# Entries of two blocks: the norm before the first block's second layer done by pairs of tiles, transposes by token tiles, and weight splits put elsewhere in the engines' orders

## The chip, the cores and the metric

One Trainium2 chip, one of its cores. The metric is device time in microseconds (us) of one execution; lower is better. The kernel before took 3221.67 us (median of 3 runs, 3217.72 to 3221.87).

## What is computed

Two blocks of two layers each, all on 512 tokens of width 1024 (four tiles of 128 tokens) and, in the first block, 256 context tokens more (tiles 4 and 5). Cut to what matters here:

```python
def first_block_layer(x, ctx):                       # twice
    h = rms_norm(x, g) * (1 + scale) + shift         # per layer, scale and shift from c (ctx likewise)
    p = h @ w_in                                     # queries, keys, values, gates, ...
    x = x + gate * (mixer(p) @ w_out)

def second_block_layer(x):                           # twice
    y = hybrid_mixer(x, ...)                         # compressed, latent and forgetting attention
    x = layer_norm(DN_ALPHA * x + y, ln_g[l, 0], ln_b[l, 0])
    y = memory_cross_attention(x, mem, xa_w_q[l], xa_w_kv[l], xa_w_o[l])
    x = layer_norm(DN_ALPHA * x + y, ln_g[l, 1], ln_b[l, 1])
    y = square(relu(x @ mlp_w_up[l])) @ mlp_w_down[l]
    x = layer_norm(DN_ALPHA * x + y, ln_g[l, 2], ln_b[l, 2])
```

All products are made at nearly full fp32 precision out of rounded fp32 parts: an operand is split into a high part (rounded) and a low part (the rest), and three products (high high, high low, low high) are added (`acc3`, L346).

## The kernel before

It is written by hand with semaphores. Each engine runs its own list of instructions in the order in which the Python code issues them; `wait_ge` makes an engine wait for a count. Most steps are functions with one part per engine (`tensor`, `dve`, `act`, `pool`), so what is issued earlier in the code comes earlier on every engine.

**Weights** come in `chunks` of up to 1 MB, loaded by SP into two raw slots in turn (`sp_chunks`, L337), each when the raw slot was freed two chunks before. A chunk is then split into high and low parts: ACT copies the rounded high part (`act_split`, L287), DVE subtracts for the low part (`dve_split`, L294), and that frees the raw slot. TensorE waits for the low part (`pe.wait_ge(*tw)`). Where the splits stand in the orders of ACT and DVE is set by `take()` (splits the chunk if that wasn't done, and the next one), `split_next()` and `plan_split`.

**Entry of a layer of the first block.** `normed` scales the tokens by their root mean square: squares on ACT, a square root on ACT, a reciprocal root made exact by small steps on DVE (L448 to L456), and six scalings of 128x1024 on DVE (L488). `modulated` transposes them by 128x128 blocks (L598) and adds scale and shift, writing `hT` as a high part (ACT L607; for the context tokens DVE L633) and a low part (DVE: L635, or L627 and L630 for every second k). It goes over the 8 k-blocks outside and over token tiles 0 to 3 and context tiles 4 and 5 inside. Then `project3` begins with `w_in`. In the first layer the projections wait for the last low part (`pe.wait_ge(*t_hT)`, L1688). In the second layer there stands a chain: `out_proj` of the first layer (its last column part n = 3 goes over six tiles: TensorE L887, DVE product with the gate L903, POOL sum L923, ACT square L917), then `barrier()` (every engine waits for all), the store of `X` to `x_rows` by POOL (L2153), `normed` for all six tiles at once, `split_next()`, `modulated`, another `barrier()` (L2180) and the first projection (L2182). `h1_low` lies where `X` lay, so DVE waits for the store before the first low part (L2173).

**Second block.** `residual` is the layer norm by token tiles; the product groups of what comes next may begin behind it (`FirstHalves`). At the second layer's start the keys' projection (`project3_T(..., begun=...)`, L2869) finishes what was begun; its evacuations are L2454 on DVE and L2462 on ACT, POOL then copies halves of the keys (L2874), and DVE's `blocks(0)` (L2909, L2915) waits for these copies before the queries' chunk is split by the next `take()`. **Memory attention** (`MemoryTiles`) is interleaved with the second residual of each layer; ahead of it stands the projection of its queries (L3560), and ahead of the evacuations of that projection stands the split of the first `mlp_w_up` chunk, issued by `FirstHalves()` through `take(False)`.

Of the kernel before, what the change touches and what calls it, by code (L numbers as in the profile page):

```python
# [8 lines left out]
F32 = mybir.dt.float32  # L9
# [85 lines left out]
def program(nc, D, out):  # L95
# [369 lines left out]
    def normed(xn, junk, loaded, squared=None):  # L465

        have = squared is not None
        squared = squared or ac.next()
# [3 lines left out]
        def act():  # L472
            a.wait_ge(*loaded)
            for t in [] if have else range(6):
# [106 lines left out]
    def modulated(l, hT, xn, tmp, ready, t_mod):  # L581
# [4 lines left out]
        for k in range(8):  # L586
            for c, ts in ((0, range(4)), (1, range(4, 6))):
                b = bank()
                work.append((k, c, ts, b, psum_free[b], mm.next(), ac.next(), dv.next()))
                psum_free[b] = work[-1][7]  # L590

        def tensor():
            for tok in ready:
                pe.wait_ge(*tok)
            for k, c, ts, b, free, full, value, low in work:
                pe.wait_ge(*free)
                for n, t in enumerate(ts):
                    m = pe.transpose(PS[:, b, n * 128:n * 128 + 128], xn[:, t, k * 128:k * 128 + 128], ident[:, :])  # L598
                m.then_inc(*mm.up())

        def act():
            a.wait_ge(*t_mod)
            for i, (k, c, ts, b, free, full, value, low) in enumerate(work):
                n = len(ts) * 128
                a.wait_ge(*full)
# [5 lines left out]
                if i >= len(tmp):  # L611
                    a.wait_ge(*work[i - len(tmp)][7])
                a.activation(tmp[i % len(tmp)][:, 0:n], PS[:, b, 0:n], ACT.Identity, bias=aff[l][:, k, c, 1:2],
                             scale=aff[l][:, k, c, 0:1]).then_inc(*al.event())

        def dve():
            v.wait_ge(*t_mod)
            for k in range(8):
                for i in (2 * k, 2 * k + 1):
                    c = i % 2  # L620
                    n = len(work[i][2]) * 128
                    v.wait_ge(*work[i][6])
                    if c == 0 and k % 2:
                        b, x = work[i][3], tmp[i % len(tmp)][:, 0:n]
                        if i >= len(tmp):
                            v.wait_ge(*work[i - len(tmp)][7])
                        v.scalar_tensor_tensor(x, PS[:, b, 0:n], aff[l][:, k, 0, 0:1], hT[0][:, k, 0:n].bitcast(F32),  # L627
# [3175 lines left out]
```

## Time and profile before

| | |
|---|---|
| median of 3 runs | 3221.67 us (3217.72, 3221.67, 3221.87) |
| profiled execution, its own time | 3218.43 us |
| its span | 3216.6 us |
| mean granted TensorE clock | 0.962 of full |
| TensorE matmul busy | 2932.8 us (91%) |
| DVE, ACT, POOL busy | 1666.1 (52%), 1068.4 (33%), 446.9 us (14%) |
| DMA | 262.00 MB, mean 81 GB/s |

A row of the timeline has the start in us from the span's start, the busy us, the engine, the line, the operation with its output and inputs, and in brackets the idle time of the engine just before, with what ended it. A duration is up to 0.1 us longer than the distance to the next row of the same engine, since consecutive instructions overlap. "PE" is TensorE's matmul, "S" the large SBUF tensor in which most data lies, "HL" the split weights, "PS" PSUM.

### The profile page before, as it was taken

The numbers are of one execution on the slowest core, as the hardware profiler recorded it, in microseconds if no ns is written. First come the engines' busy times: TensorE is split into PE (matmuls) and PEld (weight loads), VectorE is DVE, ScalarE is ACT, GpSimd is POOL, SyncE is SP. The second block draws the span as 40 slices with busy tenths as digits, with TensorE's granted clock in tenths as the row PEclk, the third lists the DMA queues.
The fourth block names the chain that finished last, engine by engine and source line by source line (L and its number), as shares of the span: only waits on it lengthen the run. The fifth ranks groups of instructions, "written<-read, shape, count | busy, mean of one in ns | idle before, by whom it ended". The sixth has DMA issues, their size and how long they took to land. (4 is left out here: it accounts for less than half of the span.)

```text
span 3216.6 us, 43502 instructions
## 1 busy us (share of the span) xinstructions
PE 2932.8 (91%) x17412; PEld 2349.5 (73%) x17412; DVE 1666.1 (52%) x3168; ACT 1068.4 (33%) x1869; POOL 446.9 (14%) x400
## 2 busy tenths in 40 slices
PE   5789989997997898999998899998899999899998
PEld 2378874787984486476888689897556688778988
DVE  6845656853577744835235542425564533653334
ACT  3333335123135521634222431311353422332231
POOL 3200013321004520402020000000131111000000
PEclk8999999998999999999999899999899999999999
DMA  5433220232223043012223222222211233132221
GB/s 166 144 123 105 92 73 1 79 92 82 73 86 56 25 113 89 1 60 66 94 84 131 66 92 93 92 92 64 66 41 33 73 99 112 53 105 92 89 94 67
DMA packets 245407, 262.00 MB, mean 81 GB/s; under 512 B 12802, under 2 KB 227954, under 8 KB 245080
## 3 DMA queue, kind: packets, MB, share of 16 engines
q1 hardware_dynamic: 227808, 203.93, 21.0%
q0 software_dynamic: 12528, 45.08, 4.0%
q10 hardware_dynamic: 4872, 10.21, 1.5%
q8 instruction: 140, 2.29, 0.3%
q14 instruction: 59, 0.48, 0.0%
HBM read 245.04 MB, written 13.11 MB: 80 GB/s over the span
## 5 line engine op out<-in xcount | busy, mean ns | idle before, releaser
L346 PE MATMUL PS<-xT,HL 128*128 128x512 f32 (+2 forms) x3552 | 800.2, 387 | 23.2 <-DVE HL L294 15.0
L294 DVE TENSOR_TENSOR HL<-S,HL 128x2048 fp32r<-128x2048 f32 (+1 forms) x204 | 422.8, 2078 | 723.4 <-ACT HL L287 721.6
L346 PEld LDWEIGHTS PS<-xT,HL 128*128 128x128 f32 (+1 forms) x3552 | 650.2, 189 | 166.0 <-DVE HL L294 16.3
L287 ACT ACTIVATE HL<-S 128x2048 fp32r<-128x2048 f32 (+1 forms) x204 | 351.4, 1728 | 732.7 <-PE PS L3620 280.1
L3620 PE MATMUL PS<-HL,hd 128*128 128x256 f32 x3072 | 377.4, 286 | 11.3 <-DVE hd L3611 11.2
L3620 PEld LDWEIGHTS PS<-HL,hd 128*128 128x128 f32 x3072 | 375.9, 195 | 13.4 <-DVE hd L3611 12.9
L1189 ACT ACTIVATE S<-S,S 128x256 f32<-128x256 f32 (+5 forms) x292 | 189.2, 648 | 210.6 <-DVE S L1130 203.3
L1224 POOL TENSOR_SCALAR S<-S,S 128x512 f32<-128x512 f32 (+4 forms) x104 | 179.0, 1721 | 419.1 <-DVE S L1145 250.0
L1092 PEld LDWEIGHTS PS<-S,S 128*128 128x128 f32 (+1 forms) x1048 | 114.5, 141 | 146.2 <-issue 39.7
L1092 PE MATMUL PS<-S,S 128*128 128x128 f32 (+1 forms) x1048 | 171.3, 291 | 44.6 <-DVE S L1158 15.9
L346 PE MATMUL PS<-h_high,HL 128*128 128x512 f32 (+1 forms) x768 | 201.2, 348 | 0.1
L346 PE MATMUL PS<-HL,h_high 128*128 128x256 f32 x1024 | 188.4, 287 | 11.7 <-DVE S L2179 5.9
L1079 PE MATMUL PS<-S 64*128 64x256 f32 (+6 forms) x736 | 162.6, 514 | 30.7 <-DVE S L1130 27.8
L346 PEld LDWEIGHTS PS<-HL,h_high 128*128 128x128 f32 x1024 | 162.7, 195 | 12.2 <-issue 6.1
L1079 PEld LDWEIGHTS PS<-S 64*128 64x128 f32 (+1 forms) x736 | 73.1, 201 | 121.6 <-DVE S L1130 62.6
L156 PE MATMUL PS<-S,S 128*128 128x256 f32 (+2 forms) x704 | 158.7, 383 | 2.7 <-DVE S L1163 1.2
L1130 DVE CUSTOM_DVE_ANT_0 S<-PS,S 128x512 f32<-128x512 f32 (+4 forms) x272 | 137.4, 535 | 40.7 <-PE PS L1079 22.7
L346 PEld LDWEIGHTS PS<-h_high,HL 128*128 128x128 f32 x768 | 135.1, 189 | 19.3 <-DVE HL L294 1.3
L156 PEld LDWEIGHTS PS<-S,S 128*128 128x128 f32 (+1 forms) x704 | 122.8, 191 | 34.2 <-issue 16.7
L346 PE MATMUL PS<-HL,h_low 128*128 128x256 f32 x512 | 146.4, 286 | 0.0
L346 PE MATMUL PS<-h_low,HL 128*128 128x512 f32 (+1 forms) x384 | 132.5, 345 | 0.0
L1103 PE MATMUL PS<-S 128*64 128x512 f32 (+4 forms) x580 | 127.0, 508 | 0.7 <-ACT S L1211 0.5
(404 smaller groups left out, 3949.2 us busy)
## 6 DMA issues: line engine op xcount, KB each, us to landing
S<-in_mlp_w_up SPq DMA_DIRECT2D x32, 1024.0 KB, 5.6
S<-in_mlp_w_down SPq DMA_DIRECT2D x32, 1024.0 KB, 5.2
S<-in_w_in SPq DMA_DIRECT2D x28, 1024.0 KB, 5.3
S<-in_w_ada SPq DMA_DIRECT2D x24, 1024.0 KB, 5.1
S<-in_w_gate SPq DMA_DIRECT2D x24, 1024.0 KB, 5.3
S<-in_w_in SPq DMA_DIRECT2D x36, 512.0 KB, 5.2
S<-in_w_mix_out SPq DMA_DIRECT2D x8, 1024.0 KB, 5.8
spectra<-S POOLq DMA_DIRECT2D x24, 256.0 KB, 4.8
```

The lines of the kernel that those rows point to most:

```text
L156: m = pe.matmul(dst, l, r, start=(i == 0), stop=(i == n - 1))
L287: m = a.activation(high, raw, ACT.Copy)
L294: m = v.tensor_tensor(low, raw, high.bitcast(F32), ALU.subtract)
L346: m = pe.matmul(dst, l[x], r[y], start=(i == 0 and j == 0), stop=(i == n - 1 and j == 2))
L1079: m = pe.matmul(scores_of(n, i, h)[:, c0:c0 + nn], lr[h][0], lr[h][1], start=True, stop=True)
L1092: m = pe.transpose(PS[0:nk, b, q * 128:q * 128 + 128], j["P"][h][q][:, pcol(q):pcol(q) + nk], ident[:, :])
L1103: m = pe.matmul(PS[h * 64:h * 64 + 64, 7, q0 * 128:q1 * 128], vals[h], PT[tr[n, i, h][2]][0:nk, q0 * 128:q1 * 128], start=(i == 0 and j["f ...
L1130: x = v.tensor_tensor_reduce(out=shaped(Pq[:, c0:c1], bias[h]), in0=shaped(ps[:, c0:c1], bias[h]), in1=bias[h], scale=1.0, scalar=m if pla ...
L1189: x = a.activation(Pq[:, c0:c1], Pq[:, c0:c1], ACT.Exp, bias=m, scale=-1.0, accum_out=st[:, k, h, i:i + 1])
L1224: g.tensor_scalar(x, x, j["st"][:, 2, 1, i:i + 1], None, ALU.mult).then_inc(*gl.event())
L3620: m = pe.matmul(PS[:, t * 2 + n // 2, (n % 2) * 256:(n % 2) * 256 + 256], hd[x][:, r * 8 + k, t * 128:t * 128 + 128], w[y][:, k, :], start ...
```

## The change

Five edits, with no arithmetic added except that three small root chains of two columns stand where one of six stood.

1. `modulated` goes over the token tiles first (8 k-blocks), then over the context tiles (8 k-blocks, two of them in one PSUM bank). It returns the token of the 8th low part; in the first layer the first projection waits for that alone, and for the last low part only after its first three tiles.
2. `out_proj` of the first layer norms the tiles by pairs (`NormPart`): mean and root of tiles 0 and 1 while tile 2 is in work, of 2 and 3 while tile 4 is, and of 4 and 5 inside `modulated`. The barrier behind it is gone; the buffers of gate rows, products and squares moved so that this holds. `X` is stored by POOL in two halves, behind the sums of tiles 1 and 3. `split_next()` stands before DVE's product of tile 1.
3. The first two projections of that layer, which need tiles 0 to 3 alone, stand ahead of the second barrier.
4. `project3_T` with `begun` calls `split_next()` ahead of its evacuations.
5. The split of the first `mlp_w_up` chunk stands in `MemoryTiles`: on ACT behind the copies of tile 0, on DVE behind the second row minimum.

```diff
+    class NormPart:
+        def plan_mean(self):
+            self.mean = dv.next()
+        def plan_rest(self):
+            self.rooted, self.done = ac.next(), dv.next()
+        def act_root(self):
+            act_sqrt(small[:, 16 + self.t0:16 + self.t1], small[:, self.t0:self.t1], self.mean)
+        def dve_mean(self):
+            mean = small[:, self.t0:self.t1]
+            v.wait_ge(*self.squared)
+            v.tensor_scalar(mean, mean, 1.0 / 1024, EPS, ALU.mult, ALU.add).then_inc(*vl.event())
+        def dve_scale(self):
...
+            dve_rsqrt(r, mean, small[:, 16 + t0:16 + t1], self.rooted).then_inc(*vl.step())
+            v.wait_ge(*vl.at)
+            for t in range(t0, t1):
+                m = v.tensor_scalar(self.xn[:, t, :], X[:, t, :], small[:, 8 + t:9 + t], None, ALU.mult)
+            m.then_inc(*vl.event())
...
-        for k in range(8):
-            for c, ts in ((0, range(4)), (1, range(4, 6))):
...
+        for c, ts in ((0, range(4)), (1, range(4, 6))):
+            for k in range(8):
...
+                if late and c and k == 0:
+                    pe.wait_ge(*late.done)
...
+                if late and i == 2:
+                    late.square()
+                if late and i == 4:
+                    late.act_root()
...
+                if late and i == 3:
+                    late.dve_mean()
+                if late and i == 4:
+                    late.dve_scale()
...
+        return work[7][8]
...
-                    if turns and t == 2:
+                    if turns and t == 2 or norms and t == 1:
                         split_next()
+                    if norms and t in (2, 4):
+                        norms[t // 2 - 1].dve_mean()
                     v.wait_ge(*full)
...
+                    if norms and t in (2, 4):
+                        norms[t // 2 - 1].dve_scale()
...
                     g.tensor_tensor(x, x, tmp[at % 2], ALU.add).then_inc(*gl.event())
+                    if norms and t in (1, 3):
+                        g.wait_ge(*added)
+                        stored(t - 1, t + 1)
...
-    pe.wait_ge(*t_hT)
+    pe.wait_ge(*t_first)
...
+    def ada1_first():
+
+        ada1()
+        pe.wait_ge(*t_hT)
...
-    t_squares = al.at
-    f = barrier()
...
     v.wait_ge(*ld_xs.all())
-    split_next()
-    modulated(1, hT, sb(BIG + 14848, 6, 1024), grid(BIG + 22016, 3, 512), [tn], t_mod1)
+    pe.wait_ge(*modulated(1, hT, xn, grid(BIG + 22016, 3, 512), [norms[1].done], t_mod1, norms[2]))
+    for c in (0, 256):
+        project3(hT, range(4), 256, lambda t, c=c: [(QKw[:, t, c:c + 256], 0, 256)])
...
     f = barrier()
-    for c in (0, 256):
-        project3(hT, range(4), 256, lambda t, c=c: [(QKw[:, t, c:c + 256], 0, 256)])
...
         w, tw, i = (begun.w, begun.tw, begun.i) if begun else early or take()
+        if begun:
+            split_next()
...
             self.dve_low(0)
             self.dve_low(1)
+            dve_split(self.next_chunk)
             self.dve_scale(0)
...
             self.act_exp(0)
             self.act_copies(0)
+            act_split(self.next_chunk)
             self.act_exp(1)
             self.act_out(0)
...
         w, tw, i = take(False)
+        plan_split(i + 1)
         ups = FirstHalves()
```

How the edits move instructions is seen at three places (line numbers are those of each kernel's own file; an "x" counts repeats). ACT from the first layer's last `out_proj` part into the second layer's `modulated`, before:

```order
L842 ACTIVATE y_high<-S_52 128x768 x8
L287 ACTIVATE HL<-S_50 128x2048 x3
L917 ACTIVATE S_52,S_49<-S_49 128x1024 x6
L442 ACT_TABLE_LOAD
L442 ACTIVATE S_49<-S_49 128x6
L287 ACTIVATE HL<-S_50 128x16x64 x2
L607 ACTIVATE h_high<-PS,S_49 128x512
L613 ACTIVATE S_52<-PS,S_49 128x512
L613 ACTIVATE S_52<-PS,S_49 128x256
```

and with the change (L977 is the square, L654 and L660 are L607 and L613 of before):

```order
L287 ACTIVATE HL<-S_50 128x2048 x3
L287 ACTIVATE HL<-S_50 128x16x64 x2
L977 ACTIVATE S_52,S_49<-S_49 128x1024 x2
L442 ACT_TABLE_LOAD
L442 ACTIVATE S_49<-S_49 128x2
L977 ACTIVATE S_52,S_49<-S_49 128x1024 x2
L442 ACTIVATE S_49<-S_49 128x2
L977 ACTIVATE S_52,S_49<-S_49 128x1024
L654 ACTIVATE h_high<-PS,S_49 128x512
L660 ACTIVATE S_52<-PS,S_49 128x512
L654 ACTIVATE h_high<-PS,S_49 128x512
L977 ACTIVATE S_52,S_49<-S_49 128x1024
```

The split (L287 with 128x16x64) went ahead of the squares, the table load and the roots between them, and the last square behind the third write of `hT`. DVE at the start of the second block's second layer, before (L2454 evacuates keys, L2909 and L2915 are `blocks(0)`):

```order
L2366 TENSOR_TENSOR xT<-PS,xT 128x4x128 x4
L2454 COPY S_52<-PS 128x512
L2909 MEMSET S_52 64x2x16
L2915 TENSOR_TENSOR S_52<-S_52 64x512
L2915 TENSOR_TENSOR S_52<-S_52 64x496
L2915 TENSOR_TENSOR S_52<-S_52 64x512
L2915 TENSOR_TENSOR S_52<-S_52 64x496
L294 TENSOR_TENSOR HL<-S_50,HL 128x16x64 x4
```

and with the change:

```order
L2443 TENSOR_TENSOR xT<-PS,xT 128x4x128 x4
L294 TENSOR_TENSOR HL<-S_50,HL 128x16x64 x2
L2533 COPY S_52<-PS 128x512
L2991 MEMSET S_52 64x2x16
L2997 TENSOR_TENSOR S_52<-S_52 64x512
L2997 TENSOR_TENSOR S_52<-S_52 64x496
L2997 TENSOR_TENSOR S_52<-S_52 64x512
L2997 TENSOR_TENSOR S_52<-S_52 64x496
L294 TENSOR_TENSOR HL<-S_50,HL 128x16x64 x2
```

The queries' chunk (two of the four L294) is split ahead of the evacuation and of `blocks(0)`. DVE around the projection of the memory's queries (L2453 evacuates it, L2772 is the row minimum, L2778 and L2783 scale the output of tile 0), before:

```order
L2366 TENSOR_TENSOR xT<-PS,xT 128x4x128 x2
L294 TENSOR_TENSOR HL<-S_50,HL 128x2048
L2453 TENSOR_SCALAR S_52<-PS 128x512
L2772 TENSOR_REDUCE S_49<-PS 128x4 x2
L2778 RECIPROCAL S_49<-S_49 128x4
L2783 TENSOR_TENSOR S_52<-PS,S_49 128x256
```

and with the change:

```order
L2443 TENSOR_TENSOR xT<-PS,xT 128x4x128 x2
L2532 TENSOR_SCALAR S_52<-PS 128x512
L2852 TENSOR_REDUCE S_49<-PS 128x4 x2
L294 TENSOR_TENSOR HL<-S_50,HL 128x2048
L2858 RECIPROCAL S_49<-S_49 128x4
L2863 TENSOR_TENSOR S_52<-PS,S_49 128x256
```

The low part of the split left the place ahead of the evacuation and stands ahead of the reciprocal.

## Rows read from the trace of the kernel before

**Rows 1.** The page, section 1: busy time and share of the span of each engine.

```profile
PE 2932.8 (91%) x17412; PEld 2349.5 (73%) x17412; DVE 1666.1 (52%) x3168; ACT 1068.4 (33%) x1869; POOL 446.9 (14%) x400
```

**Rows 2.** Timeline, first layer's `modulated` and the first projection: TensorE, ACT, DVE.

```profile
185.37 0.80 PE L346 MATMUL PS<-HL,h_high 128*128 128x256 f32 x2 [5.78 <-DVE h_low L635]
...
171.23 0.78 ACT L607 ACTIVATE h_high<-PS,S 128x512 fp32r<-128x512 f32 x1 [16.51 <-PE PS L598]
171.90 1.23 ACT L613 ACTIVATE S<-PS,S 128x512 f32<-128x512 f32 x2
...
183.38 0.74 DVE L627 SCALAR_TENSOR_TENSOR S<-PS,S,h_high 128x512 f32<-128x512 f32 x1
184.16 0.49 DVE L630 TENSOR_SCALAR h_low<-S,S 128x512 fp32r<-128x512 f32 x1
```

**Rows 3.** Timeline, second layer's entry: TensorE, then DVE, ACT, POOL.

```profile
755.01 5.64 PE L598 MATMUL PS<-S,S 128*128 128x128 f32 x30 [9.79 <-DVE S L488]
...
771.52 0.77 PE L346 MATMUL PS<-HL,h_high 128*128 128x256 f32 x2 [5.91 <-DVE S L2179]
...
745.26 0.42 DVE L903 TENSOR_TENSOR S<-PS,S 128x256 f32<-128x256 f32 x1 [2.45 <-PE PS L346]
...
750.70 4.07 DVE L488 TENSOR_SCALAR S<-S 128x1024 f32<-128x1024 f32 x6
756.54 2.36 DVE L294 TENSOR_TENSOR HL<-S,HL 128x1024 fp32r<-128x1024 f32 x2 [1.78 <-DMA x_rows<-S]
...
746.52 1.06 ACT L917 ACTIVATE S<-S 128x1024 f32<-128x1024 f32 x1 [1.71 <-POOL S L923]
...
748.13 1.28 ACT L442 ACT_TABLE_LOAD   x1 [0.46 <-DVE S L483]
...
748.31 0.77 POOL L2153 DMA_DIRECT2D x_rows<-S  x1 [1.82 <-DVE S L483]
```

**Rows 4.** Two stretches there: us, then PE, PEld, DVE, ACT, POOL busy, granted clock, DMA.

```profile
757.00:759.00 2.00, 2.00 (x11) 2.00 (x10) 2.00 (x3) 1.77 (x3) 0.00 (x0) 0.50 0.72 279
773.00:775.00 2.00, 2.00 (x11) 2.00 (x11) 1.21 (x2) 0.66 (x1) 0.00 (x0) 0.50 0.00 0
```

**Rows 5.** Timeline, start of the second block's layers (first layer 1205 to 1246, second 2212 to 2266).

```profile
1205.11 0.60 ACT L2462 ACTIVATE S<-PS 128x512 f32<-128x512 f32 x1 [11.89 <-PE PS L346]
...
1245.67 0.43 PE L2976 MATMUL PS<-S 128*64 128x31 f32 x4 [4.98 <-DVE S L2983]
...
2223.35 6.25 PE L346 MATMUL PS<-xT,HL 128*128 128x512 f32 x19 [10.66 <-DVE HL L294]
...
2265.38 0.42 PE L2976 MATMUL PS<-S 128*64 128x31 f32 x4 [4.39 <-DVE S L2983]
...
2218.03 0.09 DVE L2909 MEMSET S<- 64x32 f32 x1 [4.51 <-DMA S<-S]
...
2220.93 2.36 DVE L294 TENSOR_TENSOR HL<-S,HL 128x1024 fp32r<-128x1024 f32 x2
```

**Rows 6.** Timeline, memory attention: first layer (1762 to 1826), then second (2783 to 2839).

```profile
1763.39 1.91 ACT L287 ACTIVATE HL<-S 128x2048 fp32r<-128x2048 f32 x1 [13.25 <-DMA S<-in_mlp_w_up]
...
1768.48 2.08 PE L2713 MATMUL PS<-S,S 64*128 64x256 f32 x8 [6.19 <-DVE S L2453]
...
1825.68 0.69 DVE L2366 TENSOR_TENSOR xT<-PS,xT 128x512 fp32r<-128x512 f32 x1 [0.25 <-ACT xT L2360]
...
2784.40 1.13 PE L2713 MATMUL PS<-S,S 64*128 64x256 f32 x8 [0.78 <-ACT S L2462]
...
2794.05 0.17 DVE L2778 RECIPROCAL S<-S 128x4 f32<-128x4 f32 x1
2795.17 0.42 DVE L2783 TENSOR_TENSOR S<-PS,S 128x256 f32<-128x256 f32 x1 [0.96 <-PE PS L2733]
...
2794.16 0.48 ACT L2807 ACTIVATE S<-PS,S 128x256 f32<-128x256 f32 x1 [2.19 <-DVE S L2772]
...
2838.08 0.69 DVE L2366 TENSOR_TENSOR xT<-PS,xT 128x512 fp32r<-128x512 f32 x1 [0.25 <-ACT xT L2360]
```

More of the change, by code:

```diff
@@ L463, in load_x, with normed @@
         return ld_x.all()
-    def normed(xn, junk, loaded, squared=None):
-        have = squared is not None
-        squared = squared or ac.next()
+    def normed(xn, junk, loaded):
+        squared = ac.next()
         rooted, mean = ac.next(), dv.next()
@@ L473, in act @@
             a.wait_ge(*loaded)
-            for t in [] if have else range(6):
+            for t in range(6):
                 if t:
@@ new lines, in dve @@
+            for i, (k, c, ts, b, c0, free, full, value, low) in enumerate(work):
+                n = len(ts) * 128
+                x = tmp[i % len(tmp)][:, 0:n]
+                if late and i == 3:
+                    late.dve_mean()
+                if late and i == 4:
+                    late.dve_scale()
+                v.wait_ge(*value)
+                if c == 0 and k % 2:
+                    if i >= len(tmp):
+                        v.wait_ge(*work[i - len(tmp)][8])
+                    v.scalar_tensor_tensor(x, PS[:, b, 0:n], aff[l][:, k, 0, 0:1], hT[0][:, k, 0:n].bitcast(F32),
+                                           ALU.mult, ALU.subtract).then_inc(*vl.step())
+                    v.wait_ge(*vl.at)
+                    v.tensor_scalar(hT[1][:, k, 0:n], x, aff[l][:, k, 0, 1:2], None, ALU.add).then_inc(*vl.event())
+                    continue
+                if c:
+                    v.tensor_copy(hT[0][:, k, 512:768], x).then_inc(*vl.step())
+                    v.wait_ge(*vl.at)
+                v.tensor_tensor(hT[1][:, k, c * 512:c * 512 + n], x, hT[0][:, k, c * 512:c * 512 + n].bitcast(F32),
+                                ALU.subtract).then_inc(*vl.event())
@@ L906, in dve, with square @@
                         dve_turn_low(turns[t - 1])
+                    if norms and t in (2, 4):
+                        norms[t // 2 - 1].dve_scale()
                 if turns:
                     dve_turn_low(turns[nt - 1])
+            def square(t, added):
+                a.wait_ge(*added)
+                if t:
+                    a.wait_ge(*al.at)
+                a.activation(junk, X[:, t, :], ACT.Square, accum_out=small[:, t:t + 1]).then_inc(*al.event())
             def act():
@@ L912, in act @@
                     act_turn(turns[t])
-                for t, b, free, full, gated, added, _ in work if junk is not None and n == 3 else []:
-                    a.wait_ge(*added)
-                    if t:
-                        a.wait_ge(*al.at)
-                    a.activation(junk, X[:, t, :], ACT.Square, accum_out=small[:, t:t + 1]).then_inc(*al.step())
+                for t, b, free, full, gated, added, _ in work if norms else []:
+                    if t in (2, 4):
+                        norms[t // 2 - 1].act_root()
+                    if t == nt - 1:
+                        norms[-1].square = lambda t=t, added=added: square(t, added)
+                    else:
+                        square(t, added)
             def pool():
@@ L927, in out_proj @@
             pool()
+        return norms
     def transposed(blocks):
```

90 lines of the change are left out of this document (47 added, 43 removed).

## Prediction

> **What bounds the kernel now.** I read the page first, for the bound: TensorE's matmuls fill 91% of the span [rows 1] and its own list of work does not change, so what there is to win is its idle time and the time it runs at the lower clock. Then the waits of TensorE, for the long ones, and the timeline of every engine around each; the windows, for the granted clock; and the second block's layer 0 beside its layer 1, since these run the same instructions with different waits, so one prices the other. Five places are touched, and four of them have TensorE idle: 5.78 us ahead of the very first projection [rows 2], 9.79 and 5.91 us at the second layer's entry [rows 3], 10.66 us at the start of the second block's second layer [rows 5], 6.19 us ahead of the memory attention of its first layer, where the second layer has 0.78 at the same matmul [rows 6]. Between these places TensorE hardly stands, so an earlier start of it is kept.
>
> **Edit 1 in the first layer.** Before, projections begin at 185.37, after the last low part. Now TensorE waits for the eighth low part of the tiles. ACT makes, for two k-blocks, two high parts and one copy of 512 columns, three times 0.67 us (171.23 to 171.90), so 8.0 us for eight from 171.2, to 179.2. The eighth low part is L627 and L630, 1.27 us (183.38 to 184.65) [rows 2]. With 0.1 for the signal this is 180.6: **4.8 us earlier**. The context tiles' low parts and the next split on DVE then end near 188.3 and are wanted after three tiles, at 2.88 us each (0.43 busy and 2.45 idle of L903 [rows 3]), at 189.2: hidden, with 1 us to spare. TensorE still idles some 3.5 us ahead of it, so I count no clock gain. Ends: 3.5 (the split shows) and 6.7 (the clock stays high, 1.9 more).
>
> **Edits 1 to 3 at the second layer's entry.** Before, from the last product at 745.2 the chain runs DVE product 0.42, POOL sum, square (1.06 and its sum's read-out), mean, table load 1.28, root and five small steps (1.29 us, from the load's end at 749.41 to 750.70), six scalings 4.07, transposes at 755.01; then the store holds DVE's split until 756.54 and DVE ends at 771.4, the projection starts at 771.52 [rows 3]. Now:
> - The split (ACT 1.9 to 2.0, DVE 2.36) stands in the gap between the products of tiles 0 and 1, which is 2.45 us long: free.
> - Tile 1's square ends near 736.3, the table load near 737.5, root and small steps 738.8, two scalings (2 x 0.68) 740.2. That holds DVE's product of tile 3 by 0.7 us. Tile 3's sum 741.4, square 742.7, mean 742.9; product of tile 4, root, small steps and scalings: 745.8. TensorE begins transposing at 745.9 instead of 755.0, and at the high clock.
> - ACT's first high part follows 0.8 later, at 746.7; with the late square (1.2) among them its fourth is done at 751.8. DVE's mean and third and fourth low parts end at 753.2; root, small steps and two scalings of tiles 4 and 5 end at 755.6. They stand ahead of DVE's low parts 5 to 8, which take 2 x (0.6 + 1.27), to 759.4. TensorE starts at 759.5: **12.0 us earlier**.
> - Before, the projection began at the low clock (0.50 in 773 to 775, 11 matmuls in 2 us where 2.88 us hold 24 at the high one), about 4.5 us of it, so 2.0 us lost. Now the context's transposes run from 755.7 to 759.1 right ahead of it and are what is slow: the low clock lasted 4 us from 755.0 before, 0.50 still in 757 to 759 [rows 4]. **2.0 us gained.**
> - The barrier behind the second projection lets TensorE wait for one evacuation: 0.8 us **lost**.
> - The store: 2 MB took from 748.31 to 756.54 [rows 3]. Its second half is now issued at 741.5, 1 MB, 5 to 6 us: 747.3; DVE wants it at 747.9. If 1 us late, DVE has 1.2 us of slack before its third low part.
>
> Together **13.2 us**. Ends: 8 (each step of the pair chain 0.3 us longer, a barrier of 2) and 16 (the low clock gone, the late pair hidden).
>
> The table load took 1.28 us, and root and small steps were over 1.29 us behind it [rows 3]; nothing more fits in. The Trainium skill (ScalarE: Activation LUTs, What ACT_TABLE_LOAD costs) adds a drain of about 1.38 us to each, 2.66 in all. The row decides; by the page the pairs' chain would end 1.3 us later and the result be 3185.3.
>
> **Edit 4.** Before: DVE waits for the copies of the keys until 2218.03, does `blocks(0)`, then splits until 2223.3; TensorE stood from 2212.7 [rows 5]. Now ACT can split from 2206 to 2208, DVE until 2210.4, both idle then; the evacuations at 2210 and 2212.8 are not touched. What then follows is what layer 0 shows, where that split was made long before: from the end of the keys (ACT evacuates at 1205.1) to L2976 at 1245.67 are 40.6 us, in layer 1 from 2212.7 to 2265.38 are 52.7. **12.1 us** (10.66 of idle, the rest the low clock behind it). Layer 0 also has the next weight load and its wait of 4.98 at L2976, so that is in the price. Now this load overlaps the copies of the keys; they may come 1 to 2 us later, with 3 us of cover. Ends: 10 and 13.
>
> **Edit 5.** In layer 0 the split waits for its weights until 1763.39 (13.25 us of ACT idle), and the evacuations behind it hold TensorE to 1768.48, though the projection ended at 1762.29. In layer 1 the same matmul comes 0.78 after the end, at 2784.40. From the end of the projection to the last low part of `xT` are 63.4 us in layer 0 (1762.3 to 1825.7) and 54.5 in layer 1 (2783.6 to 2838.1) [rows 6]: 8.9 us, 5.4 of idle and 3.5 of low clock. Against that the split now stands in both layers between two links of the chain. On ACT it takes 1.92 in an idle time of 2.19: free. On DVE L2778 moves from 2794.05 behind 2.3 us of L294 to 2796.3, while L2783 stood at 2795.17 and now follows near 2796.5: 1.3 us later, and TensorE, ACT and DVE wait for each other from there on. Layer 0: 8.9 - 1.3 = **7.6 won**; layer 1: **1.3 lost**. Ends: layer 0 from 3 (no clock regained, 2 us of split) to 9; layer 1 from 0 to 4 lost. The raw slot is free later, but the load that uses it stands in SP's list behind one that waits longer.
>
> **Sum.** 4.8 + 13.2 + 12.1 + 7.6 - 1.3 = 36.4 us. The profiled execution took 3218.4: 3182.0. It lies near the lowest of the runs shown; their median is 3.2 higher, and of three two lie there. I add 2 of it: **3184.0**.
>
> **Rivals.**
> - *The clock gives nothing back* (13%). Only idle time counts: 4.8 + 12.0 - 0.8 + 10.7 + 5.4 - 2.6 = 29.5, so 3190.9. For it: TensorE still idles about 3.5 us ahead of the first projection and 6 us inside the second entry, after which it fell before. Against: layer 1's memory stage, 8.9 us shorter than layer 0's with the same work.
> - *The split tips the memory stage* (8%). TensorE's wait for L2783 grows by 1.3 us and the clock falls again there, as in layer 0 before. Each layer then pays 3.5 and 5 us more: 3192.5. The trace has light TensorE work there, which speaks for it. The Trainium skill (TensorE: Matmul & The Clock Gate, HAM oscillation) says that bursts with gaps between them start cold each time, which speaks against putting work into this chain; whether 1.3 us do it no row shows.
> - *The weight loads set the pace behind edit 4* (5%). Then its 12.1 us come back as a longer wait at L2976: 3196.1. Against: layer 0.
> - *Each table load has a drain on the chain* (5%): 3185.3.
> - *Nothing arrives* (1%): the later waits for loads absorb all four gains, and it stays within 0.2%. DVE's and ACT's shares (52%, 33%) speak against it.
> - *Slower than before* (3%): with fewer gaps TensorE is granted the low clock over long stretches. Every us there costs half a us, so to outdo 36.4 us and 6.4 more it takes 86 us at half clock more than now, a mean of 0.935 instead of 0.962: 3228. Against: the stretches without idle all show 1.00.
>
> The forecast itself has 65%. The range that holds 8 in 10 takes in the two clock cases and the upper ends of two terms: 3176 to 3196. A measurement of this kernel can tell about 0.2% from no change, 6.4 us. Faster by more: 0.95; within it: 0.02; slower by more: 0.03.
>
> **What would show it.** First projection near 180.6; second layer's transposes within 1 us of the last product and its projection about 12 us earlier on the same count; no wait of TensorE for L294 at the keys, L2976 about 12 us sooner behind them; the first L2713 of layer 0 within 1 us of the projection's end, and L2783 of both layers about 1.3 us later against its first L2713. The prediction is wrong if DVE's product of tile 3 holds TensorE, if the store ends after 749, or if the gaps turn up again at the next wait for weights.

## The result and the profile after

| | before | after |
|---|---|---|
| median | 3220.49 us (4 runs, 3217.72 to 3221.87) | 3184.64 us (4 runs, 3178.59 to 3185.66) |
| ratio, 95% interval | | 0.9886, 0.9869 to 0.9903 |
| profiled execution, its span | 3218.43, 3216.6 us | 3184.11, 3182.3 us |
| mean granted clock | 0.962 | 0.965 |
| idle time of TensorE, sum of the brackets in its timeline | 274.0 us | 244.9 us |

35.9 us less by the medians, 34.3 between the two profiled executions. TensorE's idle time fell by 29.1 of them. Its busy time, for the same 17412 matmuls, fell by 5.5 on the page [rows 1]; that goes with the higher mean clock. Of all executions in this document one, 4270.8 us at a mean clock of 0.626 (in a_no1), was slow and is left out; the clock of the others is 0.959 to 0.972.

```profile
PE 2927.3 (92%) x17412; PEld 2348.3 (74%) x17412; DVE 1667.8 (52%) x3180; ACT 1069.1 (34%) x1871; POOL 448.1 (14%) x401
```

The lines of the kernel after: L598 of before is now L640, L635 is L679 or L684, L903 is L964, L917 is L977, L923 is L994, L2713 is L2793, L2783 is L2863, L2976 is L3058.

First layer's entry, timeline of TensorE [rows 2], the transposes of before, then the kernel after:

```profile
170.45 2.84 PE L598 MATMUL PS<-S 128*128 128x128 f32 x24
```

```profile
169.80 5.67 PE L640 MATMUL PS<-S 128*128 128x128 f32 x44
176.06 0.66 PE L640 MATMUL PS<-S 128*128 128x128 f32 x4 [0.59 <-DVE h_low L679]
180.07 0.80 PE L346 MATMUL PS<-HL,h_high 128*128 128x256 f32 x2 [3.36 <-DVE h_low L679]
```

From the first transpose to the first projection are 10.3 us, where before had 14.9 (170.45 to 185.37). So 4.65 of the 5.3 us by which the projection comes earlier are the edit's; 0.65 were there ahead of the transposes.

Second layer's entry, timeline of TensorE, then DVE, ACT and POOL [rows 3]:

```profile
747.95 3.72 PE L640 MATMUL PS<-S,S 128*128 128x128 f32 x32 [0.98 <-DVE S L606]
757.84 3.65 PE L640 MATMUL PS<-S,S 128*128 128x128 f32 x16 [6.17 <-DVE S L606]
761.32 0.79 PE L346 MATMUL PS<-HL,h_high 128*128 128x256 f32 x2
...
785.62 0.47 PE L346 MATMUL PS<-HL,h_high 128*128 128x256 f32 x2 [0.63 <-PE PS L346]
...
750.29 0.69 DVE L684 TENSOR_TENSOR h_low<-S,h_high 128x512 fp32r<-128x512 f32 x1 [2.06 <-ACT S L660]
756.28 1.42 DVE L606 TENSOR_SCALAR S<-S 128x1024 f32<-128x1024 f32 x2
...
738.20 1.28 ACT L442 ACT_TABLE_LOAD   x1
739.49 0.20 ACT L442 ACTIVATE S<-S 128x2 f32<-128x2 f32 x1
748.71 0.78 ACT L654 ACTIVATE h_high<-PS,S 128x512 fp32r<-128x512 f32 x1 [1.70 <-PE PS L640]
...
743.58 0.74 POOL L2194 DMA_DIRECT2D x_rows<-S  x1 [0.30 <-POOL S L994]
```

TensorE transposes 0.98 us after its last product (9.79 before); the context's transposes wait 6.17 us for the late pair's scalings (L606); the projection follows them at once. DVE's first low part waits for ACT, not for the store. Windows there (columns as in [rows 4]): the low clock of the two levels, 0.50, has the context's transposes, and is over 0.9 us after the projection has begun (0.95 in 762 to 764).

```profile
756.00:758.00 2.00, 0.16 (x1) 0.19 (x2) 1.93 (x5) 2.00 (x4) 0.00 (x0) 0.50 0.00 0
758.00:760.00 2.00, 2.00 (x10) 2.00 (x10) 1.97 (x5) 0.89 (x2) 0.00 (x0) 0.50 0.03 8
760.00:762.00 2.00, 2.00 (x10) 1.77 (x10) 1.93 (x6) 1.27 (x3) 0.00 (x0) 0.50 0.00 0
762.00:764.00 2.00, 2.00 (x18) 2.00 (x18) 1.90 (x7) 1.70 (x3) 0.00 (x0) 0.95 0.00 0
```

Keys of the second block's second layer [rows 5]: ACT splits while it would idle, the copies come after a longer wait, and TensorE is at L3058 at 2233.10, with nothing in its rows where 10.66 us stood.

```profile
2187.20 2.01 ACT L287 ACTIVATE HL<-S 128x1024 fp32r<-128x1024 f32 x2 [1.44 <-DVE xT L2443]
...
2193.32 0.69 DVE L2533 COPY S<-PS 128x512 f32<-128x512 f32 x1 [1.62 <-PE PS L346]
2200.65 0.09 DVE L2991 MEMSET S<- 64x32 f32 x1 [6.64 <-DMA S<-S]
...
2233.10 0.31 PE L3058 MATMUL PS<-S 128*64 128x31 f32 x4 [4.21 <-DVE S L3065]
```

Memory attention [rows 6], layer 0, and the same matmuls of layer 1:

```profile
1749.59 1.13 PE L2793 MATMUL PS<-S,S 64*128 64x256 f32 x8 [0.99 <-DVE S L2532]
...
1759.24 2.28 DVE L294 TENSOR_TENSOR HL<-S,HL 128x2048 fp32r<-128x2048 f32 x1
1761.44 0.17 DVE L2858 RECIPROCAL S<-S 128x4 f32<-128x4 f32 x1
1761.76 0.42 DVE L2863 TENSOR_TENSOR S<-PS,S 128x256 f32<-128x256 f32 x1 [0.15 <-PE PS L2813]
...
2749.68 1.13 PE L2793 MATMUL PS<-S,S 64*128 64x256 f32 x8 [0.78 <-ACT S L2541]
2762.33 0.69 PE L2819 MATMUL PS<-S,S 128*128 128x128 f32 x2 [0.59 <-DVE S L2863]
```

6.19 us of idle time are 0.99. The split ends where `dve_scale` wants to begin, and L2863 comes 12.2 us behind the first L2793, where layer 1 of before had 10.8.

**One thing did not fit.** Set beside each other matmul by matmul, the kernel after is 5.3 us ahead at the first projection and level with the kernel before (0.1 behind) at 355 us: the first edit's gain was gone long before the second layer. No row of TensorE shows new idle time there. The windows around its gaps of 2.8 us ahead of the modulation products (L510, now L509) do show something. Before, then after twice:

```profile
295.00:305.00 10.00, 7.21 (x38) 5.02 (x37) 6.70 (x9) 2.48 (x2) 0.00 (x0) 0.83 0.35 107
```

```profile
290.00:300.00 10.00, 7.22 (x35) 5.29 (x34) 7.14 (x10) 2.48 (x2) 0.00 (x0) 0.73 0.34 107
338.00:348.00 10.00, 7.18 (x31) 5.22 (x30) 8.26 (x11) 2.55 (x3) 0.00 (x0) 0.72 0.33 107
```

A mean clock of 0.83 over 10 us costs 1.7 us of full-speed work, 0.73 and 0.72 cost 2.7 and 2.8. (Both stretches at the low clock run on past the end of their window in the kernel after.) Matmul by matmul the lead falls from 5.3 to 4.6 us during the first projection, to 3.0 behind the gap near 294 and to -0.1 behind the one near 341. Whether the edit brings that about, or chance, is the first question for the experiments.

### The profile page after: what moved, and what is told of

Read it like the earlier page. It is cut to its first block, busy times and chain, and to the rows that moved or that the text cites. A ratio compares the mean times of both kernels' runs of the same rounds, so it can differ in the third digit from the quotient of the medians.

```text
span 3182.3 us, 43510 instructions
## 1 busy us (share of the span) xinstructions
PE 2927.3 (92%) x17412; PEld 2348.3 (74%) x17412; DVE 1667.8 (52%) x3180; ACT 1069.1 (34%) x1871; POOL 448.1 (14%) x401
## 4 chain that ended last, share of the span: by engine, by line
PE 55%; DVE 10%; issue 2%; ACT 2%; DMA 1%; POOL 0%; DVEq 0%; SPq 0%; ACTq 0%; POOLq 0%
PE PS L346 29%; PE PS L3703 11%; PE PS L156 3%; PE PS L1167 2%; PE PS L1154 2%; PE PS L3604 2%; PE PS L1178 2%; DVE S L1205 2%; DVE S L1233 1%; DVE S L2591 1%; DVE HL L294 1%; DVE S L1226 1%; DVE S L2587 1%; ACT HL L287 1%; PE PS L3366 1%
## 5 line engine op out<-in xcount | busy, mean ns | idle before, releaser
L346 PE MATMUL PS<-xT,HL 128*128 128x512 f32 (+2 forms) x3552 | 796.0, 385 | 12.5 <-DVE xT L2443 4.7
L294 DVE TENSOR_TENSOR HL<-S,HL 128x2048 fp32r<-128x2048 f32 (+1 forms) x204 | 423.2, 2079 | 692.8 <-ACT HL L287 692.7
L287 ACT ACTIVATE HL<-S 128x2048 fp32r<-128x2048 f32 (+1 forms) x204 | 351.4, 1728 | 719.7 <-PE PS L3703 282.8
L3703 PE MATMUL PS<-HL,hd 128*128 128x256 f32 x3072 | 378.8, 287 | 11.3 <-DVE hd L3694 11.2
L3703 PEld LDWEIGHTS PS<-HL,hd 128*128 128x128 f32 x3072 | 377.3, 196 | 13.4 <-DVE hd L3694 12.9
L156 PEld LDWEIGHTS PS<-S,S 128*128 128x128 f32 (+1 forms) x704 | 122.3, 191 | 34.7 <-issue 14.9
```

The lines of the kernel that those rows point to most:

```text
L156: m = pe.matmul(dst, l, r, start=(i == 0), stop=(i == n - 1))
L287: m = a.activation(high, raw, ACT.Copy)
L294: m = v.tensor_tensor(low, raw, high.bitcast(F32), ALU.subtract)
L346: m = pe.matmul(dst, l[x], r[y], start=(i == 0 and j == 0), stop=(i == n - 1 and j == 2))
L3703: m = pe.matmul(PS[:, t * 2 + n // 2, (n % 2) * 256:(n % 2) * 256 + 256], hd[x][:, r * 8 + k, t * 128:t * 128 + 128], w[y][:, k, :], start ...
```

## Experiments

Twelve experiments in three series (first the four on the kernel before, then a_same to a_k, then a_same2 to a_best). All of one series share a chip and its runs of the kernel before (medians 3214.2, 3214.5 and 3215.6 us, 43 runs from 3205.8 at a mean clock of 0.965 to 3222.3 at 0.961). "Means" below are those of the timed runs; an "error" is the standard error, and one of a difference has to be doubled for an interval of 95%.

### One edit at a time on the kernel before

**b_e1**, the first edit in the first layer alone: the new `modulated` for l = 0 only, with

```diff
-    pe.wait_ge(*t_hT)
+    pe.wait_ge(*t_first)
...
+    def ada1_first():
+        ada1()
+        pe.wait_ge(*t_hT)
```

> The kernel before with the first edit in the first layer alone (k-blocks inside token tiles, projection starts after the eighth low part). Theory A, the start is kept: first projection near 180.1 to 180.6 instead of 185.4, and the execution 4.8 us shorter, 3215.7 beside 3220.5. Theory B, the clock takes it back: the first projection comes as early, but the gaps of 2.8 us ahead of the modulation products between 270 and 400 (L510 of before) are followed by the low clock more often than before (granted 0.86 and 0.83 in 280 to 300 and 340 to 360 in the changed kernel, 0.96 and 1.00 before), and at 420 us nothing of the 4.8 is left: within 1 us of the kernel before. Theory C: which gaps are followed by the low clock changes from execution to execution; then the trace may show either, and the median over the rounds shows 2 to 4 us.

Measured: 3213.45 us beside 3214.24, ratio 0.9995 (0.9986 to 1.0004): between 4.5 us less and 1.3 more.

```profile
178.79 0.79 PE L346 MATMUL PS<-HL,h_high 128*128 128x256 f32 x2 [3.36 <-DVE h_low L711]
```

The projection starts early as in the kernel after. Of the gaps between 270 and 400, two have a low spell behind them, a short stretch at the lower of the two clock levels (clock 0.83 over the 10 us around 292, and again around 382), and the stretch from the first projection to the product near 425 us takes 246.3 us (244.4 before). By the times, between nothing and 4.5 us arrives: the 4.8 of theory A lie just outside, the 2 to 4 of theory C inside.

**b_entry**, the second layer's entry alone: the kernel after with the old `modulated` for l = 0, `pe.wait_ge(*t_hT)` ahead of the first projection, and edits 4 and 5 taken out as in the diff.

> The kernel before with the second layer's entry of the change alone (norm by pairs, transposes by tiles, store by halves, first barrier gone, two projections ahead of the second barrier). By the prediction 13.2 us shorter: 3207.3. By the count of idle time alone (no clock regained) 11.2: 3209.3. By the trace of the changed kernel: transposes 1.0 us behind the last product, the context's transposes 6.2 us of idle later, projection 14.3 to 14.8 us after the last product instead of 26.3, so 12 us at this place.

Measured: 3201.74 us, ratio 0.9967 (0.9955 to 0.9979), so 6.8 to 14.5 us. In the trace the two timelines are 12.0 us further apart at the projection and 12.9 at 952 us.

**b_e4**, the fourth edit alone:

```diff
         w, tw, i = (begun.w, begun.tw, begun.i) if begun else early or take()
+        if begun:
+            split_next()
```

> The kernel before with the fourth edit alone (the split of the queries' chunk ahead of the keys' evacuations in layer 1 of the second block). By the prediction 12.1 us shorter: 3208.4. By idle time alone 10.7: 3209.8. Rival, the weight loads set the pace: the wait at L2976 grows and less than 3 us arrive, above 3217. The trace of the changed kernel showed the two timelines 13.0 us further apart behind this place and 1 to 3 us more by the end of the attention that follows.

Measured: 3200.96 us, ratio 0.9964 (0.9952 to 0.9976), 7.7 to 15.4 us. TensorE's wait at L2976 is as long as before (4.39 there), so the weight loads set no pace:

```profile
2251.41 0.43 PE L2978 MATMUL PS<-S 128*64 128x31 f32 x4 [4.26 <-DVE S L2985]
```

**b_e5**, the fifth edit alone (`plan_split(i + 1)`, and `act_split`, `dve_split` in `act_first`, `dve_first`).

> The kernel before with the fifth edit alone (split of the next chunk inside the memory attention, both layers). By the prediction 7.6 won in layer 0 and 1.3 lost in layer 1, 6.3 in all: 3214.2. By idle time alone (5.4 won, 2.6 lost) 2.8: 3217.7. Rival, the split in the chain lets the clock fall in layer 1: nothing won, 3220. Trace: layer 0 from its first scores to the last low part 52.9 us instead of 57.3, layer 1 52.9 instead of 53.7 or so.

Measured: 3210.37 us, ratio 0.9987 (0.9978 to 0.9997), 1 to 7 us. Both theories lie inside; the trace decides, below.

```profile
1766.26 1.13 PE L2714 MATMUL PS<-S,S 64*128 64x256 f32 x8 [0.99 <-DVE S L2453]
```

### The kernel after, less or more

**a_same**, the kernel after itself.

> The changed kernel itself, on the chip of this series, as the measure for its variants. If the four parts tried alone add up (0.8, 10.3, 12.0 and 4.4 us by the means), it is 27.5 us shorter than the kernel before; if they help each other, 36 as in the first comparison (ratio 0.9886).

Measured: 3179.3 us, ratio 0.989 (0.9875 to 0.9904): 35.4 us. The four parts tried alone give 28.0 by their ratios; each has a 95% interval of some 3 to 4 us to either side, the sum of 7, so that the 7 us between are no proof that the parts help each other.

**a_no1**, the first edit undone in the first layer.

> The changed kernel with the first layer's entry as before (first projection behind the last low part of all k-blocks). Theory A, the early start is kept: 4.8 us slower than the changed kernel. Theory B, given back to the low clock between 270 and 400 us: within 1.5 us of it, with the first projection 5 us later in the trace. Trace, for both: how many of the gaps of 2.8 us near 275, 297, 343 and 388 are followed by the low clock; one costs some 2.5 us.

Measured: 3183.94 us (five executions), ratio 0.9905 (0.9889 to 0.9921). Means: 3184.6 (error 1.6) against 3179.3 (1.0), so 5.2 slower with an error of 1.8. This speaks for theory A, b_e1 against it, and a gain of 2 to 4 us lies inside both intervals: the times alone do not settle it.

**a_no3**, the first two projections behind the barrier:

```diff
-    for c in (0, 256):
-        project3(hT, range(4), 256, lambda t, c=c: [(QKw[:, t, c:c + 256], 0, 256)])
...
     f = barrier()
+    for c in (0, 256):
+        project3(hT, range(4), 256, lambda t, c=c: [(QKw[:, t, c:c + 256], 0, 256)])
```

> The changed kernel with its first two projections of the second layer behind the barrier again. The barrier then waits for DVE's last low part of the context tiles, at 766.6 in the trace of the changed kernel, and opens 0.5 to 1 us later, so TensorE starts near 767.4 instead of 761.3: 6 us slower, and 0.8 us come back where the barrier stands now: 5 us slower in all by idle time, 7 with the clock that falls in the longer gap. Rival, DVE's splits and evacuations behind the barrier were the limit anyway: under 2 us slower.

Measured: 3185.8 us, ratio 0.9913 (0.9899 to 0.9927). Means: 7.7 us slower, error 1.9. TensorE waits 5.49 us for the last instruction ahead of the barrier on DVE:

```profile
750.62 3.53 PE L640 MATMUL PS<-S,S 128*128 128x128 f32 x16 [6.17 <-DVE S L606]
759.63 0.77 PE L346 MATMUL PS<-HL,h_high 128*128 128x256 f32 x2 [5.49 <-DVE S L2256]
```

From the modulation product at 430 us to 952 us it takes 515.1 us, 5.5 more than the mean in the table below (3.3 more than the longest of it), with 5.7 us more of idle time: by this one trace the third edit is worth some 5.5 of the 13 at this entry.

**a_k**, waits by k-block:

```diff
+                if lows and t == tiles[0]:
+                    for k in range(8):
+                        pe.wait_ge(*lows[k])
+                        l, r = cols3(x, k, t * 128, 128), cols3(w, k, 0, n)
+                        for j, (p, q) in enumerate(THREE):
+                            m = pe.matmul(PS[:, b, 0:n], l[p], r[q], start=(k == 0 and j == 0), stop=(k == 7 and j == 2))
```

> The changed kernel, with TensorE waiting for each k-block's low part in the first tile of the first projection (both entries) instead of for the eighth at its start. The low parts come every 0.9 us (2 in 1.8 us), a k-block of a tile takes 0.36 us: the first tile should end some 0.4 to 0.8 us behind the eighth low part instead of 2.9 us, so 2.1 to 2.5 us gained at each entry, in the second layer perhaps 1 us less, since 3.6 us of context transposes then stand ahead of it. Theory A (gains are kept): 3 to 4.5 us faster than the changed kernel. Theory B (what is gained at the first entry is given back to the clock): 1 to 2 us faster.

Measured: 3175.76 us, ratio 0.9877 (0.9858 to 0.9895); means 4.2 us under a_same, error 3.1. The first entry gains 2.7 us against the trace of a_same, 2.9 against that of the kernel after; the second gains 0.2 or less:

```profile
179.04 0.50 PE L718 MATMUL PS<-HL,h_high 128*128 128x256 f32 x2 [0.47 <-DVE h_low L679]
...
187.15 2.00 PE L509 MATMUL PS<-HL,c 128*4 128x256 f32 x16 [1.72 <-DVE HL L294]
...
749.47 3.65 PE L640 MATMUL PS<-S,S 128*128 128x128 f32 x16 [6.18 <-DVE S L606]
752.77 0.77 PE L718 MATMUL PS<-HL,h_high 128*128 128x256 f32 x2
```

At the first entry TensorE's wait of 3.36 us for the eighth low part has become one of 0.47 in the middle of the first tile, the clock is 1.00 in 180 to 190 (0.66 before, 0.73 after), and the next limit appears: 1.72 us for the split. At the second, the context's transposes at the low clock last until the eighth low part is there anyway.

### The low clock, by trace

Each profile of these kernels is a sample of the same stretches. The table splits the profiled executions at matmuls that all have; each entry is the mean length in us, in brackets lowest to highest and the number of traces (a_k and a_best, whose first tile has waits of its own, are left out, and so is a kernel in the stretch that it changes by itself).

| stretch, edit | without | with | gained | of it idle | forecast |
|---|---|---|---|---|---|
| start to product at 430 (1) | 430.0 (426.9 to 432.5, 5) | 426.1 (424.3 to 429.9, 6) | 3.9 | 3.8 | 4.8 |
| from there to 952 (1 to 3) | 522.8 (521.3 to 525.1, 4) | 509.6 (507.5 to 511.8, 7) | 13.1 | 8.8 | 13.2 |
| to the down projection of layer 0 at 1913 (5) | 959.4 (957.8 to 960.9, 4) | 953.0 (951.0 to 954.9, 8) | 6.4 | 5.7 | 7.6 |
| to 2304 (4) | 391.6 (390.9 to 393.1, 4) | 377.4 (376.7 to 378.4, 8) | 14.2 | 10.1 | 12.1 |
| first scores of layer 1 (2784) to 2927 (5) | 141.9 (141.3 to 142.8, 5) | 143.3 (143.1 to 143.6, 7) | -1.4 | -1.2 | -1.3 |

3.9 + 13.1 + 6.4 + 14.2 - 1.4 = 36.2, beside 35.4 to 36.7 by the three ratios. In the last three stretches a_k and a_best could be counted as well, and they are at the edges: 951.9 and 957.8 with the edit, 373.1 and 378.2 with it, 143.1 with it and 139.0 without. With them the gains would be 6.0, 14.5 and -1.8.

Of the first edit's 4.65 us, 0.5 to 0.9 are given back at once: from the first projection the product at 200 us takes 14.6 to 14.7 us in the five traces without the edit and 15.1 to 15.6 in the six with it, since the low clock that follows the wait then meets more of the projection (5.3 us of it in the first profile of the kernel after, 3.7 in that of the kernel before). What happens further on differs from trace to trace. From the first projection to the product at 430 the idle time is 12.0 to 12.1 us in every one of these traces, so that only the clock tells them apart: 244.3 to 247.6 us without the edit, 246.1 to 249.8 with it. Of its gaps near 272, 294, 340 and 385 the second is followed by a low spell in every trace, the first in three, in kernels with and without the edit, the third in the first profile of the kernel after alone. The fourth is followed by one in four of the seven traces with the edit (a_k among them) and in none of the five without. The means, 245.6 and 246.8, so differ by 1.2 us. About half of it is what the projection itself gives back; the rest is the fourth gap, and four of seven against none of five can still be chance. That it gave all 5.3 back in the first profile was chance, since the same program took 246.2 us in a_same and 249.8 there.

**a_same2**, the kernel after once more.

> The changed kernel a third time, as the measure for the three variants beside it: ratio to the kernel before 0.989 (0.9886 and 0.9890 so far). Its trace is one more sample of which gaps between 270 and 400 us the low clock follows: at least one of the four, and the stretch from the first projection to the product at 430 us takes 246 to 250 us.

Measured: 3178.8 us, ratio 0.9888 (0.987 to 0.9905). Low spells behind the second and fourth gap; 246.2 us. It was at the foot of the range that was expected.

**a_fill**, work in the gaps:

```diff
+        for _ in range(20 if (l, n) in ((1, 4), (1, 5), (1, 7), (1, 9)) else 0):
+            pe.transpose(PS[:, b, 0:128], ident[:, :], ident[:, :])
         pe.wait_ge(*tw)
```

> The changed kernel with 20 transposes of the identity (into the bank that the modulation product then overwrites) in each of the four gaps of 2.8 us at the modulation products near 272, 294, 341 and 388. Theory A, the low clock follows the idle time: none of the four is followed by it, clock 1.00 all through 265 to 400, and the stretch from the first projection to the product at 430 takes 243 us instead of 246 to 250: 1.5 to 5 us faster than the changed kernel, if nothing else moves. Theory B, the clock falls for another reason (the small products themselves, or a fixed point of time): it still falls at one or two of them, time as the changed kernel's. If the 20 transposes take more than the gap, each costs the rest.

Measured: 3178.07 us, ratio 0.9886 (0.9869 to 0.9904); means 0.4 under a_same2, error 2.1. Timeline of one gap, and the windows at all four:

```profile
289.64 2.35 PE L507 MATMUL PS<-S 128*128 128x128 f32 x20
292.58 1.99 PE L511 MATMUL PS<-HL,c 128*4 128x256 f32 x16 [0.59 <-DVE HL L294]
```

```profile
265.00:275.00 10.00, 9.41 (x71) 8.14 (x71) 6.87 (x11) 4.00 (x4) 0.00 (x0) 1.00 0.33 107
287.00:297.00 10.00, 9.41 (x73) 8.16 (x72) 8.12 (x13) 3.23 (x3) 0.00 (x0) 1.00 0.32 104
334.00:344.00 10.00, 9.38 (x61) 7.65 (x59) 8.21 (x11) 2.24 (x2) 0.00 (x0) 1.00 0.31 105
378.00:388.00 10.00, 9.37 (x61) 7.64 (x60) 8.32 (x11) 2.30 (x2) 0.00 (x0) 1.00 0.33 107
```

The clock is 1.00 at all four, and the stretch takes 243.3 us as theory A said. The second gap carries the proof, since it is followed by a low spell in all twelve traces that have it; filled, here and in a_best, it is not. So the idle time ahead of the product is what lets the clock fall, not the product. The gain of 3 us over this stretch does not show in the times: the same profile has 811.3 us from 952 to the memory attention, where a_same2 has 807.6, by the clock again (idle 71.2 and 71.4). What is won at one gap can be lost at others by chance, and a few runs do not tell 1 to 3 us from that.

**a_l0**, the fifth edit in layer 0 only:

```diff
-        plan_split(i + 1)
+        if l == 0:
+            plan_split(i + 1)
```

> The changed kernel with the fifth edit kept in layer 0 and undone in layer 1. By the prediction 1.3 us faster, seen in the trace between the first scores of layer 1 and the first matmul of the down projection: 142 us (141.3 to 142.8 in the traces without the fifth edit) instead of 143.2 (143.1 to 143.5 with it). Rival: in layer 1 the split has to wait for its weights too since the load starts later, and it is slower by 1 to 5 us.

Measured: 3175.92 us, ratio 0.988 (0.9862 to 0.9898); means 1.3 under a_same2, error 1.9. The stretch takes 141.3 us, 2 us less than with the edit. The rival came near:

```profile
2745.08 1.92 ACT L287 ACTIVATE HL<-S 128x2048 fp32r<-128x2048 f32 x1 [7.81 <-DMA S<-in_mlp_w_up]
2749.47 0.60 ACT L2541 ACTIVATE S<-PS 128x512 f32<-128x512 f32 x1 [2.47 <-PE PS L346]
```

ACT does wait 7.8 us for the weights, but is done 2.5 us before the evacuation wants it.

**a_best**, all three together.

> All three together: k-block waits at both entries, filled gaps, the fifth edit in layer 0 alone. If they add up: 3 + 3 + 1.2, so 7 us faster than the changed kernel, ratio to the kernel before 0.9868. If only the k-block waits hold: 0.988.

Measured: 3174.73 us, ratio 0.9877 (0.9858 to 0.9896); means 3.4 under a_same2, error 1.8. The clock is 1.00 at the filled gaps and the lowest of its runs is no lower than that of a_same2 (3173.6 and 3173.4). By its median it is the fastest version, by less than the forecast 7 and at the edge of what so few executions tell; by the ratio it is level with a_k (0.9877 both), so that the two other changes are not shown to add anything.

## Why the prediction was right

The forecast, 3184.0, is 0.6 us from the median. The mechanism held at each of the five places; that the total is so close is in part luck. By the table's means the terms miss by 0.9, 0.1, 1.2, 2.1 and 0.1 us, and these misses cancel to 0.2. Beside that, the level itself moves: this one kernel had medians of 3184.6, 3179.3 and 3178.8 us on three occasions, the kernel before 3220.5, 3214.5 and 3215.6. Term by term:

- **Edit 1, 4.8 us.** The first projection came 5.3 us earlier (180.07 for the 180.6 foreseen), 4.65 of them from the transposes on. What is kept on average is 3.9 by the traces, with b_e1 below that and a_no1 above; 0.4 of this average arose ahead of the transposes, so it is rather 3.5. The step "between these places TensorE hardly stands, so an earlier start of it is kept" was wrong as a premise: the five places hold 38 of the 274 us of idle time, and behind this one stand four gaps of 2.8 us, behind which the clock differs from one execution to the next.
- **Edits 1 to 3 at the second entry, 13.2.** Measured 13.1. From the last product, transposes were foreseen after 0.7 and came after 0.98 us; from the transposes, the first high part after 0.8 (0.76), the context's transposes after 9.8 (9.89), the projection after 13.6 (13.37); the barrier costs 0.63 for 0.8. From the last product, the product at 800 us comes 55.1 to 55.7 us later in the four traces without the edits and 42.0 to 42.4 in the seven with them: 13.2 less. The 2.0 us for the clock do not follow from "11 matmuls" and "24" as written, which give 1.5; they follow from the spacing of three matmuls, 0.64 us at the low clock and 0.36 at the high one. DVE's product of tile 3 was held for 0.8 us (0.7 foreseen), and TensorE did not wait for it. The split was not quite free: beside POOL's sum it took 2.89 us for 2.36 (last section), and DVE's product of tile 1 came 0.3 us late, hidden. The term was right as a sum and less so in its halves: 8.8 of it is idle time and 4.3 the clock, where 11.2 and 2.0 were written down, since part of what counted as saved time had been transposes at the low clock.
- **The store.** Its second half was issued at 743.58 and landed 4.4 us later, at 748.0; DVE was done with its last product at 748.2, and the first low part waited for ACT's copy until 750.29.
- **The table load.** The load ended at 739.48 and the root began at 739.49; the instruction ahead of the load ended at 738.17 and the load began at 738.20. The drain that the Trainium skill (ScalarE: Activation LUTs, What ACT_TABLE_LOAD costs) adds appears neither behind the load nor ahead of it, and the rival that rested on it falls.
- **Edit 4, 12.1.** Measured 14.2, and this is the term that was mis-sized most. The comparison with layer 0 ended at L2976 (now L3058); up to there it gave 12.7 (52.7 us from the end of the keys' products before; 40.0 after, from 2193.1, just ahead of DVE's copy at 2193.32, to 2233.10), and 12.9 by the mean of all traces. The other 1.5 us arose behind it, up to 2304, by the clock: in the first profiles the kernel before has 0.50 over the better part of 2263 to 2272, the kernel after only over 2233 to 2237, and there the traces overlap (36.9 to 39.8 us without the edit, 36.4 to 39.1 with it). Over the whole stretch all eight traces with the edit are at least 12.5 us shorter than all four without. The copies of the keys came 2 us later (a wait of 6.64 for 4.51) and were covered, as foreseen.
- **Edit 5, layer 0, 7.6.** Measured 6.4. The local count of the first two profiles was 8.2 by 1797 us and 7.5 by 1826, where the forecast counted; by 1913 it was 6.7. The forecast took the clock's part, 3.5 us, from one trace: from the end of the projection to 1826 the four traces without the edit take 61.6 to 64.1 us, the kernel before's the 64.1, and the eight with it 56.6 to 58.0, which is 6.3 less by the means.
- **Edit 5, layer 1, 1.3 lost.** Measured 1.4, and 2 got back in a_l0.
- **2 us added for the level of the runs.** The median lay 0.5 above the profiled execution; between the two profiled executions the gain was 34.3 for the 36.4 forecast.

Of the rivals, "the clock gives nothing back" priced idle time alone at 29.5 us; TensorE's idle time fell by 29.1, and the other 5 us between the two profiles came from the clock (9 of the 36.2 by the means of the table). "The split tips the memory stage" did not happen: with the split, TensorE's wait for L2863 in layer 1 (`[... <-DVE S L2863]`, at L2819) is 0.59 us in three traces, where its matmuls before it ran at the low clock, and 1.8 to 2.3 in five, where they ran at the high one, and both give a stretch of 143.1 to 143.6 us. Without it the wait is 0.59 at either clock. The split's 1.3 us is so, as these rows read, a floor that DVE sets, not a new gap that slows what follows. The loads set no pace behind edit 4 (b_e4). In "slower than before" the mean clock is wrong: 86 us more at half clock take 43 us off the work of 3217, which makes 0.949 of 0.962, not 0.935; nothing else hangs on it.

## What to carry to other kernels

Price a moved wait by idle time, which came back as 29.1 us in one pair of profiles and 27.2 by the means of the table, for the 29.5 counted, and treat what the clock adds as a mean with a spread: a single profile can show the whole gain of a small edit swallowed, or doubled. Before believing either, compare the same stretch over several traces of kernels that share it; that cost nothing here, and told 4 us in 430 where the times could not. And when waits are taken from the front of a chain, look at what else fills the time until its end: at the second entry 3.6 us of transposes at the low clock stood beside DVE's last low parts, so that finer waits gained next to nothing there.

## What the runs showed of the hardware

- A gap of 2.8 us of TensorE, the same in every trace, is followed by the clock's lower level (1.2 of 2.4 GHz) in some executions and not in others of one program (near 341 in the first profile of the kernel after, not at the same gap in a_same). With 2.35 of the 2.8 us filled with transposes the clock stayed high at all four places, in two traces (a_fill, a_best); the gap near 294 had been followed in all twelve traces without that. The Trainium skill (TensorE: Matmul & The Clock Gate, HAM oscillation) tells of bursts that each start cold behind a gap; here the trace agrees for the cause, but not every gap is paid for.
- DVE's product of two columns, L450, takes 0.16 us, and 0.71 when POOL's sum runs, ending with it, in all ten traces with the new entry. Timeline of DVE and of POOL, kernel after:

```profile
745.14 0.71 DVE L450 TENSOR_TENSOR S<-S 128x2 f32<-128x2 f32 x1
745.88 0.16 DVE L452 TENSOR_TENSOR S<-S 128x2 f32<-128x2 f32 x1
...
745.10 0.73 POOL L994 TENSOR_TENSOR S<-S,S 128x256 f32<-128x256 f32 x1 [0.78 <-DVE S L964]
```

  In the other direction a sum of POOL that meets DVE's split took 1.65 us for 0.73, in the same ten traces, and the split 2.89 for 2.36:

```profile
733.12 1.65 POOL L994 TENSOR_TENSOR S<-S,S 128x256 f32<-128x256 f32 x1 [2.14 <-DVE S L964]
...
732.95 2.89 DVE L294 TENSOR_TENSOR HL<-S,HL 128x1024 fp32r<-128x1024 f32 x2
```

  The Trainium skill (SBUF — State Buffer, SBUF: two separate sides) has the reason: DVE with two inputs from SBUF and GpSimd take a shared pair of ports in turns, each for its whole instruction. The rows agree. On the chain of the second pair this was 0.55 us, more than the 0.3 by which the transposes came later than foreseen.
- How much of a low spell follows a gap, and what in an execution decides it, stayed open; no run here separates it.
